# A ring of six gathered rows in place of eight, and seven loads of query weights in place of nine

## The reference

```
h = rmsnorm(x) ; q,k,v,... = h @ w_in
x = x + concat(sparse_attention, retention) @ w_out
# PEER: per token and head (8 heads), 16 of 16384 experts
q  = rmsnorm(x) @ w_query                       # 1024 x 2048
s1, s2 = q[:, :, 0] @ keys1.T, q[:, :, 1] @ keys2.T
e_idx, gate = top 16 of the sums of both top 16s, softmax of their scores
act = gelu(sum_d exp_u[e_idx] * h)
x = x + sum over heads and k of gate * act * exp_v[e_idx]
y = rmsnorm(x)
```

## Time and profile before

| | |
|---|---|
| time, three runs | 1155.89, 1156.53, 1156.76 us |
| median | 1156.53 us |
| span of the profiled execution, first to last instruction | 1155.1 us |
| moved by DMA | 458.68 MB, mean 397 GB/s |
| of it by the gathers' queue (q0) | 402.68 MB |
| busy: PE / DVE / POOL / ACT | 76% / 71% / 48% / 39% |
| gathers, issue to landing, median | 12.4 us |

### The profile page before, as it was taken

The page is one execution under the profiler, slowest core; times in us unless marked ns, Lnnn a source line. Parts: engine busy times, 40 slices in busy tenths (PEclk is TensorE's granted clock), DMA queues, the critical chain, the costliest instruction groups (busy, mean ns, idle before and its releaser), DMA issues.

```text
span 1155.1 us, 12183 instructions
## 1 busy us (share of the span) xinstructions
PE 875.5 (76%) x3735; PEld 397.5 (34%) x3740; DVE 816.8 (71%) x2123; ACT 448.7 (39%) x1413; POOL 553.4 (48%) x437
## 2 busy tenths in 40 slices
PE   8999988997888857665677768587656667666556
PEld 6748644443333424232233333143222122221111
DVE  2426877876686979996777785757886777767544
ACT  2121444433443424433554663343333333333334
POOL 0002444552554745553564563655474554555443
PEclk9999999999997988897898899888898778877779
DMA  9902999999999999999999999999999999999996
GB/s 378 401 1 78 427 424 426 426 426 429 394 422 428 406 427 426 376 421 423 428 427 424 426 427 427 425 427 425 419 380 426 426 427 426 427 426 427 428 426 274
DMA packets 67079, 458.68 MB, mean 397 GB/s; under 512 B 8387, under 2 KB 10179, under 8 KB 15686
## 3 DMA queue, kind: packets, MB, share of 16 engines
q0 software_dynamic: 55888, 402.68, 83.3%
q1 hardware_dynamic: 10982, 54.97, 11.7%
q10 hardware_dynamic: 144, 0.26, 0.1%
HBM read 453.59 MB, written 3.24 MB: 395 GB/s over the span
## 4 chain that ended last, share of the span: by engine, by line
DMA 41%; PE 26%; DVE 16%; POOL 7%; issue 6%; ACT 3%; SPq 0%; POOLq 0%; DVEq 0%
DMA rows<-in_uv,ids 39%; PE ps L581 25%; DVE rows L1991 8%; POOL rows L520 5%; POOL work L505 1%; ACT work L1212 1%; DMA rows<-in_w_qi 1%; ACT wgt L1212 1%; DMA wt<-in_w_q 1%; DMA rows<-in_uv,last_ids 1%; PE ps L584 1%; DVE top L1581 1%; ACT zact L1212 1%; DVE wt L1585 1%; DVE work L1714 0%
## 5 line engine op out<-in xcount | busy, mean ns | idle before, releaser
L520 POOL DMA_INDIRECT rows<-in_uv,ids x380 | 454.1, 1195 | 471.0 <-PE ps L581 402.7
L581 PE MATMUL ps<-rows,work 128*64 128x512 f32 x1536 | 463.1, 733 | 262.5 <-ACT work L1212 261.8
L1991 DVE CUSTOM_DVE_ANT_0 rows<-rows,wt 128x1024 f32<-128x1024 f32 x256 | 314.0, 1227 | 168.5 <-DMA rows<-in_uv,ids 165.0
L1212 ACT ACTIVATE zact<-zdot 128x1 f32<-128x1 f32 x384 | 77.6, 202 | 555.7 <-DVE zdot L1991 555.2
L581 PEld LDWEIGHTS ps<-rows,work 128*64 128x64 f32 x1536 | 107.1, 155 | 525.2 <-ACT work L1212 366.1
L1991 DVE CUSTOM_DVE_ANT_0 rows<-rows,masks 128x1024 f32<-128x1024 f32 x128 | 157.3, 1231 | 51.4 <-DMA rows<-in_uv,ids 48.5
L581 PE MATMUL ps<-wt 128*128 128x128 f32 (+7 forms) x599 | 155.9, 414 | 0.9 <-DMA wt<-in_w_kv 0.9
L1212 ACT ACTIVATE work<-pair,wgt 128x64 f32<-128x64 f32 x384 | 133.5, 348 | 12.5
L1212 ACT ACTIVATE wgt<-zact,gates 128x1 f32<-128x1 f32 x384 | 113.1, 295 | 12.4
L581 PEld LDWEIGHTS ps<-wt 128*128 128x128 f32 (+2 forms) x604 | 89.2, 192 | 55.1 <-issue 46.9
L581 PEld LDWEIGHTS ps<-work,wt 128*128 128x128 f32 (+1 forms) x664 | 85.1, 203 | 55.7 <-issue 55.7
(11 more groups left out here) (168 smaller groups left out, 679.0 us busy)
## 6 DMA issues: line engine op xcount, KB each, us to landing
wt<-in_w_q SPq DMA_DIRECT2D x8, 2048.0 KB, 12.2
rows<-in_uv,ids POOLq DMA_INDIRECT x380, 12.4
rows<-in_w_out SPq DMA_DIRECT2D x2, 2048.0 KB, 32.2
wt<-in_w_out SPq DMA_DIRECT2D x2, 2048.0 KB, 11.8
wt<-in_ckv SPq DMA_DIRECT2D x16, 256.0 KB, 11.0
x<-in_x SPq DMA_DIRECT2D x5, 512.0 KB, 8.6
rows<-in_w_qi SPq DMA_DIRECT2D x1, 2048.0 KB, 12.9
wt<-in_w_qa SPq DMA_DIRECT2D x1, 2048.0 KB, 11.9
```

Of the source, the lines that this page charges most:

```text
L520: pool.indirect_dma_start(row[s], None, a["uv"], bass.IndirectOffsetOnAxis(ap=ids[:, own(n // KP).start + n % KP:own(n // KP).start + n % ...
L581: return nc.tensor.matmul(out, lhsT, rhs, start=start, stop=stop)
L1212: return nc.scalar.activation(*args, **kw)
L1991: V.tensor_tensor_reduce(row[s][:, 0:D], row[s][:, 0:D], h2r[t][:, n % 2, :], 1.0, 0.0, ALU.mult, ALU.add, zdot[:, s:s + 1]).then_inc(dott ...
```

## The change

The ring has six places, `G = 6`, while `rows` keeps its size of eight. The two places left out are the ones that load 0 fills, and that slab now stays there to the end. The waits of the gathers follow `G`: gather n waits for the pair that holds n - 6. The wait of gather 6 for the queries of units 0 and 1 is gone.

With the first slab resident, tile 1 and tile 2 read it there. Which unit reads which load is a new table. The slab that ScalarE copies is now load 4 (slab 2). Tile 1 reads loads 3, 4, 0, 5; tile 2 reads loads 5, 0, the copy and 6. Two loads of 2 MB go: the one that SP issued between the first loads of cached keys (`load_ckv`), and the last one. ScalarE's last copy waits for the store of the retention state, which used to be ordered otherwise.

```diff
-G = 8
+G = 6
@@
-        rows = sb("rows", [P, G, 2 * D])
+        rows = sb("rows", [P, 8, 2 * D])
@@
-        PLACE = (4, 5, 6, 7, 0, 1, 2, 3)
+        PLACE = (4, 5, 6, 7, 0, 1)
@@ def w_q(k):
-            return slot(wt[:, 0 if k < 7 else k - 4, :])
+            return slot(wt[:, 0 if k < 6 else 3, :])
@@
-        Q_LOADS = (0, 1, 2, 3, 2, 1, 0, 2, 3)
+        Q_LOADS = (0, 1, 2, 3, 2, 1, 3)
@@ def q_load(u):
-            return (6, HELD, 7, 8)[h // 2] if t == 2 else (0, 3)[t] + h // 2
+            return ((0, 1, 2, 3), (3, 4, 0, 5), (5, 0, HELD, 6))[t][h // 2]
@@ def load_q(k):
-                elif 0 < k < 7:
-                    sp.wait_ge(q_ps, [u for u in range(UNITS) if q_load(u) < k][-1] + 1)
-                if k == 6:
+                elif 1 < k < 6:
+                    sp.wait_ge(q_ps, [u for u in range(UNITS) if q_load(u) == k - 1][-1] + 1)
+                if k == 5:
                     sp.wait_ge(q_held, 5)
@@
             load_ckv(1)
-            load_q(5)
             sp.wait_ge(mt_ps, TILES)
...
                 if b == 4:
-                    load_q(6)
+                    load_q(5)
             sp.wait_ge(pv_ps, ATT[2] + STREAMS)
             sp.dma_start(x[:, 2, :], a["x"][2]).then_inc(x_again[2], 16)
-            load_q(7)
+            load_q(6)
...
-            sp.wait_ge(wout, 2 * TILES)
-            load_q(8)
@@ def gather(n):
-                if n == 6:
-                    pool.wait_ge(q_ps, 2)
                 if n >= G:
                     pool.wait_ge(acc, (n - G) // 2 + 1)
@@ def keep_queries():
-                act.wait_ge(q_in[0], 16 * 6)
-                slab = w_q(5)
+                act.wait_ge(q_in[0], 16 * 5)
+                slab = w_q(4)
...
+                        act.wait_ge(ss_out, 16)
```

More of the change, by code:

```diff
@@ L278, in build @@
         w_in = {n: sem("w_" + n) for n in ("kv", "qi", "qa", "vb", "qkb", "gb", "out0", "out1", "out2", "out3")}
-        q_in = [sem(f"q_in{i}") for i in range(4)]
+        q_in = [sem(f"q_in{i}") for i in range(2)]
         x_in = [sem(f"x_in{t}") for t in range(TILES)]
@@ L404, in load_q @@
                     sp.wait_ge(qa_ps, 3)
-                elif 0 < k < 7:
-                    sp.wait_ge(q_ps, [u for u in range(UNITS) if q_load(u) < k][-1] + 1)
-                if k == 6:
+                elif 1 < k < 6:
+                    sp.wait_ge(q_ps, [u for u in range(UNITS) if q_load(u) == k - 1][-1] + 1)
+                if k == 5:
                     sp.wait_ge(q_held, 5)
-                dst = wt[:, 0 if k < 7 else k - 4, :] if k else at(rowf, SLOT, SLOT)
-                sp.dma_start(dst, a[f"w_q{Q_LOADS[k]}"]).then_inc(q_in[max(0, k - 6)], 16)
+                dst = wt[:, 0 if k < 6 else 3, :] if k else at(rowf, SLOT, SLOT)
+                sp.dma_start(dst, a[f"w_q{Q_LOADS[k]}"]).then_inc(q_in[k // 6], 16)
             load_q(0)
@@ L801, in query_part @@
                     else:
-                        pe.wait_ge(q_in[max(0, k - 6)], 16 * (k + 1 if k < 7 else 1))
+                        pe.wait_ge(q_in[k // 6], 16 * (k + 1 if k < 6 else 1))
                 e, c0 = part // 4, part % 4 * 2
```

## The result

The changed kernel takes **1254.05 us** (median of 4 runs, 1248.79 to 1263.8), the kernel before beside it 1156.64 (4 runs, 1155.89 to 1157.96). The ratio is 1.0846, with a 95% interval of 1.0800 to 1.0892. It is slower by 97 us where 39 were forecast, and outside the range. The profiled execution is the slowest of the four, 1263.8 us with a span of 1262.0; stage by stage it is compared with the span before, 1155.1.

The account below looks back on a forecast made before the run. The prediction took a flat DMA rate of 427 GB/s as the bound. Stage losses of 14 + 10 + 4 + 8 + 10 and 3 at the start made 49 us, less 9.8 for the slabs: +39, 1195 us, range 1163 to 1222.

Parts of the forecast that it names:

- The bound now: Whole gather stretch: DMA moves bytes at one flat rate, 427 GB/s, the queue is never empty, so waits to issue cost nothing.
- I take 7.9: Ring of six: mean issue to landing in a nearly empty queue is 7.9 us, chosen between 6.8 and 8.9.
- The return unchanged: Landing to next issue does not get shorter with the ring: 7.5 us late, 10.1 and 11.3 in the early stages.
- The stages: Five stretches of gathers lose 14, 10, 4, 8 and 10 us, the third before the slabs' 9.8 come off.
- My own column for 8.9: With 8.9 us to landing the five stages lose 33, 28, 18, 19 and 25 us; the change is +116, 1273 us.
- The start, 3 us: First gathers: six go out where eight did, gather 6 waits for the first pair, and the queue's gap costs 3 us.
- The slabs, -9.8: Two slab loads of 2.1 MB removed, 4.9 us of all DMA engines each: 9.8 us off while the queue stays full.
- a rival inside the forecast: Removed slab loads: saved bytes save nothing since a dry queue has room for them; 1201 us, no chance of its own.
- Deep enough: Ring of six: landing takes 6.8 us or simply gets 5 us shorter, so six places suffice; 1150 us, chance 7%.
- Small loss: Landing near 7.3 us: late stages keep pace or lose 3 us, early ones lose 15; 1158 to 1175, chance 20%.
- TensorE slows or a floor near 8.9: Late gathers: low-clock matmuls lengthen the return, +40 over the forecast, or landing nears 8.9 us; 1235 us, chance 15%.
- Priced at nothing: ScalarE's wait for the retention state's store, load 5's new place, and TensorE's waits for `in_w_q` cost nothing.

Follow-up runs that it names:

- Half dots: Each dot over 512 of 1024 elements: 1206.17 us in the changed kernel, 1157.07 us in the kernel before with its ring of eight.
- Gathers alone with a return: All but gathers left out, with made work between a pair's landing and its next issue: 2.49 us a gather with eight places, 2.79 with six.
- the wait of seven: Kernel before, places and slab loads kept, but gather n waits for the pair that holds n - 7: 1170.34 us.
- the wait alone: Kernel before with its eight places and nine slab loads, but gather n waits for the pair that holds n - 6: 1258.53 us.
- The gathers alone: All but gathers left out, a set number in flight, freed one by one: 5.78 us a gather with one, 2.89 with two, 2.50 with three.

## Why the prediction was wrong, point by point

- **The bound now** (flat DMA rate, return free): right. Half dots in the ring of eight change nothing.
- **"I take 7.9"**: this is the step that failed. In the changed ring issue to landing is 8.9 us: 8.8 and 8.9 as medians in the two late stages above that show landings. For the changed kernel itself no view lists it, as a few of the landings' semaphore events are missing from its trace. Those that are there (the last one of each gather) give a mean of 8.9 for the 86 late gathers. The earlier trace rows had the number: in its long dry stretch the median was 8.9, and I took the minimum of that stretch, 7.9, because it agreed with one restart. Behind it was a wrong picture. I thought of a queue that is nearly empty, which takes 5.5 us. But a ring at 2.5 to 2.75 us a gather has more than three in flight, and then each gather stands in line: 7.2 us if freed one by one, 8.2 in pairs, 8.9 in this kernel (8.9 over 2.75 is 3.2 in flight). What adds the last 0.7 is open. Gathers alone with a return show it neither for uneven laps nor for exponentials; they take random rows, though, where the kernel takes the chosen ones, and that was not varied. Nor is 8.9 one number for the whole kernel: the same events give 9.6, 9.6, 9.7, 8.9 and 8.9 in the five stages, so while the rest of the layer is done beside the gathers the term was too small by some 1.7, not by 1.0.
- **The return unchanged** (7.5 late): nearly. Six times 2.75 less 8.9 is 7.6. The lap is 16.5 us where 15.4 were computed, and 1.0 of the 1.1 is the time to landing. In the two early stages the same working gives returns of 9.0 and 9.0, where 10.1 and 11.3 were put in. That fits my guess that part of it is rows that lie and wait; the guess itself was not tested.
- **The stages.** Forecast 14, 10, -6, 8, 10; measured 27, 14, 14, 15, 25. My own column for 8.9 had 33, 28, 18, 19 and 25, and 8 for the third once the slabs' 9.8 are taken off. The late one is met. The first two came out lower, since the return gave way more than a longer landing took; the third came out higher, since landing took 9.7.
- **The start, 3 us**: 9. Gather 6 is not the only one that waits; each of the next pairs goes out when the pair after it did in the ring of eight. Gather 10 is issued at 142.2, where gather 12 was before, in place of 133.2. With the wait of seven it is 1.4 us late.
- **The slabs, -9.8**: right in a full queue (10.5); in a short one 4.5 by the medians, which can't be told from nothing. I had this as a rival inside the forecast.
- **The rivals.** Deep enough: no. Small loss: no. TensorE slows or a floor near 8.9, 15%, with 1235: its second half, the floor, was the truth, and my own upper end of 1273 was closer than the forecast. TensorE's part of the *increase* is small, from 799 to 860 ns a matmul, eight of them two abreast: 0.24 us a lap. The sign that I gave for it, pairs of over 3 us nearly all the time, did not come either: 23 of 42 late pairs in the trace, where 15 of 42 were before. The range stopped at 1222 though its own text worked out 1273; that was the second mistake.
- **Priced at nothing** (the store, load 5, `in_w_q`): right. TensorE has no wait for `in_w_q` and ScalarE none for the store, and the wait alone costs all of the loss.
- **The Trainium skill's rule.** "DMA: Bandwidth & Descriptors", section "Anatomy of one DMA — SWDGE (gpsimd) path", gives 4.4 us for one gather by the estimate in the prediction. The gathers alone don't agree: one with nothing beside it takes 5.5 us from issue to landing.

## What to carry to other kernels

A ring is deep enough when places times the pace at full rate is more than landing plus return. The landing time to put in is that of a queue with as many in flight as full rate needs, freed in the groups in which the ring frees them. It is neither the time in an empty queue nor the minimum of a dry stretch. In the late stage here that is 8.9 + 7.5 = 16.4 us: seven places at 2.46 us give 17.2 and just suffice, six give 14.7 and don't. Before shortening a ring, measure it with a wait alone: seven cost 13 us here and six 101, and that small edit would have told it before any slab was moved. Once the limit is passed, time on the way from landing to issue, free until then, has a price: half a microsecond of every dot was worth 48 us here.

## What the runs showed of the hardware

- Two gathers of 1.049 MB in flight keep the DMA engines 96% busy at 353 GB/s; three give 419. The busy share does not show a short queue, the rate does.
- One such gather alone takes 5.5 us from issue to landing, and the second in flight adds nothing to that (5.5 again, at 2.89 us a gather). The third adds 1.7 us, and each further one 2.5: 7.2, 9.7, 12.2, 14.7 for three to six.
- In a ring of six with a return of 9 us, places freed in pairs take 1.2 us longer from issue to landing than places freed one by one (8.3 and 7.1 us).
- Six bf16 matmuls after each pair brought the granted clock of the late stage from 0.74 to 0.98 and the pairs' matmuls from 860 to 629 ns.
